# Building a state-space layer's Toeplitz matrices by a trip through DRAM, with the skip term folded into the lag matrix

## What is computed

```
def s5_mixer(h, w_in, ..., d_skip, w_glu):
    u = h @ w_in
    # per group of 16 channels, a complex state of 64:
    #   x[t] = a * x[t-1] + B @ u[t];   y[t] = Re(C @ x[t])
    y = y + d_skip * u
    g = gelu(y)
    val, gate = split(g @ w_glu, 2)
    return val * sigmoid(gate)
```

## Time and profile before

| | us |
|---|---|
| median of 3 runs | 2933.1 (2932.86 to 2935.42) |
| the profiled execution | 2935.41 |
| its span in the profile | 2933.6 |
| PE busy in the span | 2619.5 |
| DVE busy | 1939.3 |
| POOL busy | 1675.2 |
| ACT busy | 830.6 |

### The profile page before, as it was taken

One profiled execution on the slowest core, in us unless ns is written; L12 is line 12 of the kernel. 1 busy time (PEld: TensorE's weight loads), 2 busy tenths in 40 slices (PEclk: granted clock), 3 DMA queues, 4 the chain that ended last, 5 costly groups with the idle time before them and its releaser, 6 DMA issues.

```text
span 2933.6 us, 32517 instructions
## 1 busy us (share of the span) xinstructions
PE 2619.5 (89%) x9882; PEld 1218.3 (42%) x9882; DVE 1939.3 (66%) x3952; ACT 830.6 (28%) x1809; POOL 1675.2 (57%) x1024
## 2 busy tenths in 40 slices
PE   7989888888878888887778999999999988999999
PEld 3554333333333333332333684444444445444444
DVE  8847777777777777777877683666336596566523
ACT  3423222222222222222234461222112246222101
POOL 5544444444444444444535877777776651677776
PEclk9999999999999999999999979999999999999999
DMA  4259999999999999999972322233322320233332
GB/s 137 71 201 414 421 421 417 414 417 412 417 415 412 412 409 418 415 401 422 420 312 69 105 74 88 93 101 105 118 93 88 116 73 8 79 100 102 120 98 81
DMA packets 133244, 696.18 MB, mean 237 GB/s; under 512 B 30011, under 2 KB 31324, under 8 KB 67196
## 3 DMA queue, kind: packets, MB, share of 16 engines
q0 software_dynamic: 73728, 536.90, 44.5%
q1 hardware_dynamic: 59388, 157.74, 16.6%
HBM read 686.72 MB, written 7.86 MB: 237 GB/s over the span
## 4 chain that ended last, share of the span: by engine, by line
PE 34%; DMA 24%; POOLq 16%; DVE 12%; issue 7%; ACT 3%; DVEq 2%; POOL 1%; SPq 0%; ACTq 0%
DMA R<-expert_uv_dram,idx 24%; PE bank L586 20%; PE bank L814 9%; POOLq L2736 8%; POOLq L2734 7%; DVE R L2164 3%; POOL R L2761 1%; DVE Z L2186 1%; DVE xt L2449 1%; ACT Z L1437 1%; DVE R L1900 1%; PE bank L983 1%; PE bank L1170 1%; DVE R L2176 0%; DVE ci L2110 0%
## 5 line engine op out<-in xcount | busy, mean ns | idle before, releaser
L814 PE MATMUL bank<-R,Z 128*128 128x512 f32 x2048 | 971.4, 619 | 230.8 <-ACT Z L1437 225.3
L2761 POOL DMA_INDIRECT R<-expert_uv_dram,idx x512 | 596.5, 1165 | 723.7 <-PE bank L814 675.5
L586 PE MATMUL bank<-R 128*128 128x512 f16 (+1 forms) x3936 | 865.8, 381 | 6.6 <-DVE R L1882 2.6
L2164 DVE SCALAR_TENSOR_TENSOR R<-R 128x1024 f32<-128x1024 f32 x512 | 622.8, 1222 | 198.0 <-DMA R<-expert_uv_dram,idx 196.9
L814 PEld LDWEIGHTS bank<-R,Z 128*128 128x128 f32 x2048 | 381.6, 195 | 803.8 <-issue 420.5
L2733 POOL TENSOR_TENSOR R<-wring,beat 128x1024 f16<-128x1024 f32 (+2 forms) x219 | 447.2, 2042 | 394.7 <-PE bank L586 349.4
L586 PEld LDWEIGHTS bank<-R 128*128 128x128 f16 (+1 forms) x3936 | 383.7, 98 | 483.4 <-issue 25.3
L2735 POOL TENSOR_TENSOR R<-wring,R 128x1024 bf16<-128x1024 f32 (+2 forms) x219 | 510.2, 2330 | 31.8 <-issue 0.3
L1437 ACT ACTIVATE Z<-consts,R 128x128 f32<-128x128 f32 x512 | 177.7, 394 | 321.3 <-DVE R L2176 316.8
L586 PE MATMUL bank<-Z,R 128*128 128x512 f16 x1104 | 239.9, 379 | 1.5 <-POOLq L2736 1.5
L1430 ACT ACTIVATE R<-R 128x2 f32<-128x2 f32 x256 | 52.1, 204 | 608.3 <-DVEq L2166 607.9
(11 more groups left out here) (369 smaller groups left out, 2521.2 us busy)
## 6 DMA issues: line engine op xcount, KB each, us to landing
wring<-up_dram SPq DMA_DIRECT2D x88, 512.0 KB, 3.5
wring<-down_dram SPq DMA_DIRECT2D x32, 704.0 KB, 4.2
wring<-ple_dram SPq DMA_DIRECT2D x16, 640.0 KB, 3.9
wring<-w_in_dram SPq DMA_DIRECT2D x18, 512.0 KB, 3.5
R<-expert_uv_dram,idx POOLq DMA_INDIRECT x512
wring<-glu_dram SPq DMA_DIRECT2D x16, 512.0 KB, 4.2
Z<-w_q_dram SPq DMA_DIRECT2D x11, 512.0 KB, 8.0
wring<-ple_a_dram SPq DMA_DIRECT2D x8, 640.0 KB, 5.9
```

The costliest lines, as they stand in the source:

```text
L586: mm = pe.matmul(bank[:, :], low(w) if i else w, low(v) if j else v, start=(start and c == 0 and p == 0), stop=(stop and c == n - 1 and p ...
L814: mm = pe.matmul(banks[2 * par + c][:, :], diag[:, k % 4, :], pairs[:, slot, 1, c * SEQ:(c + 1) * SEQ], start=(k == 0), stop=(k == TOPK - 1))
L2164: dot = ve.scalar_tensor_tensor(pairs[:, slot, 0, :], pairs[:, slot, 0, :], 1.0, ntok[:, T, :], ALU.mult, ALU.mult, accum_out=act[:, par, ...
L2761: po.indirect_dma_start(pairs[:, slot, :, :].rearrange("p a b -> p (a b)"), None, A["expert_uv"], bass.IndirectOffsetOnAxis(idx[:, n % 2, ...
```

## The change

The shift products and their evictions are gone. The lag matrix goes from SBUF to DRAM (`lagD`) behind seven blocks of zeros, and one DMA with overlapping rows reads it back as Tg: row (j, c) starts j blocks further on. Powers 0 to 7 are now made in rising order, so that the u chunks are stored in reversed order, by eight DMAs per tile in place of one. The skip vector becomes a 16 x 128 matrix per tile, added to lag 0 by one product with 16 rows of the identity, ahead of the eight narrow products. `total` on DVE goes, and the gelu reads the landed y. The zeros are set in stage `final_a`, and two DMAs put them into DRAM. The copy that made the shift matrix is gone.

```diff
+        LAGS = (2 * CH - 1) * GC
+        lagD = nc.dram_tensor("lagD", [2, GC, GT, LAGS], F32, kind="Internal")
...
 SP, stage ssm_in
                     stream(name)
+                    for i, (at, n) in enumerate(((0, 2), (2, 2), (4, 4))):
+                        sp.dma_start(skips[i], A["ssm_skip"][:, at:at + n, :]).then_inc(d_loaded, 16)
+                    sp.wait_ge(ri_ready, NORM["ssm_in"] + 1)
+                    for slot in range(2):
+                        sp.dma_start(bass.AP(lagD, slot * P * LAGS, [[LAGS, P], [1, (CH - 1) * GC]]), pad)\
+                          .then_inc(d_loaded, 16)
...
-                        sp.dma_start(flat(uD, n).rearrange("(s p j) -> p s j", p=P, j=NCH),
-                                     uperm[:, n, :].rearrange("p (s j) -> p s j", j=NCH)).then_inc(u_stored[n % 2], 16)
+                        for i in range(CH):
+                            back = flat(uD, n)[(CH - 1 - i) * P * NCH:(CH - i) * P * NCH]
+                            sp.dma_start(back.rearrange("(p j) -> p j", j=NCH), uperm[:, n, i * NCH:(i + 1) * NCH])\
+                              .then_inc(u_stored[n % 2], 16)
...
 SP, stage ssm
                     stream("glu", ahead=True)
+                    def lags_out(n):
+                        sp.wait_ge(h_ev, n + 1)
+                        if n >= 2:
+                            sp.wait_ge(t_loaded, 16 * (n - 1))
+                        sp.dma_start(bass.AP(lagD, n % 2 * P * LAGS + (CH - 1) * GC,
+                                             [[GC, CH], [GT * LAGS, GC], [LAGS, GT], [1, GC]]),
+                                     hmat.rearrange("p (g m) -> p g m", m=GC)).then_inc(h_stored, 16)
+                    def lags_back(n):
+                        sp.wait_ge(h_stored, 16 * (n + 1))
+                        if n == 0:
+                            sp.wait_ge(d_loaded, 80)
+                        else:
+                            sp.wait_ge(t_loaded, 16 * n)
+                        if n >= 2:
+                            sp.wait_ge(y_mm, n - 1)
+                        sp.dma_start(Tg[:, n % 2, :, :],
+                                     bass.AP(lagD, n % 2 * P * LAGS, [[GC, CH], [GT * LAGS, GC], [LAGS, GT], [1, P]]))\
+                          .then_inc(t_loaded, 16)
+                    for n in range(2):
+                        lags_out(n)
+                        lags_back(n)
                     for n in range(KT):
+                        if n + 2 < KT:
+                            lags_out(n + 2)
+                            lags_back(n + 2)
                         sp.wait_ge(yo_ev, n + 1)
                         sp.dma_start(yD.ap()[n], ysb[:, n % 2, :]).then_inc(y_stored, 16)
...
 PE, stage ssm
                         if n:
-                            pe.wait_ge(te_ev, 2 * n - 1 + half)
+                            pe.wait_ge(bt_ev, 2 * n - 1 + half)
...
+                    pe.matmul(banks[2][:, 0:P], ident[0:GC, :], skip[n], start=True, stop=False)
                     for g in range(GT):
                         mm = pe.matmul(banks[2][:, g * GC:(g + 1) * GC], row(gmat[:, n % 2, g, :, :]),
-                                       Cm[:, n * GT + g, :], start=True, stop=True)
+                                       Cm[:, n * GT + g, :], start=False, stop=(g == GT - 1))
...
-                def output_matrices(n):
-                    pe.wait_ge(h_ev, n + 1)
-                    for half in range(2):
-                        pe.wait_ge(bt_ev, 2 * n + 1 + half)
-                        for j in range(4):
-                            at = (CH - 1 - half * 4 - j) * GC
-                            mm = pe.matmul(banks[half][:, j * P:(j + 1) * P], shifts[:, at:at + P], hmat,
-                                           start=True, stop=True)
-                        mm.then_inc(t_mm, 1)
...
                 def outputs(n):
-                    pe.wait_ge(te_ev, 2 * n + 2)
+                    pe.wait_ge(t_loaded, 16 * (n + 1))
...
 ACT, stage ssm
                     ac.wait_ge(h_mm, n + 1)
                     if n:
-                        ac.wait_ge(t_mm, 2 * n)
+                        ac.wait_ge(h_stored, 16 * n)
                     ac.activation(hmat, banks[2][:, 0:P], ACT.Copy).then_inc(h_ev, 1)
-                def output_matrices(n):
-                    if n >= 2:
-                        ac.wait_ge(y_mm, n - 1)
-                    for half in range(2):
-                        ac.wait_ge(t_mm, 2 * n + half + 1)
-                        ac.activation(Tg[:, n % 2, :, half * SEQ // 8:(half + 1) * SEQ // 8]
-                                      .rearrange("p g (t c) -> p t g c", c=GC),
-                                      banks[half][:, :].rearrange("p (t g c) -> p t g c", g=GT, c=GC),
-                                      ACT.Copy).then_inc(te_ev, 1)
...
 DVE
+                ve.memset(pad, 0.0)
...
-                ve.tensor_copy(shifts[:, 0:P], ident)
-                ve.memset(shifts[:, P:], 0.0)
...
-                def total(n):
-                    ve.wait_ge(tile_landed[n], 48)
-                    ve.scalar_tensor_tensor(uperm[:, n, :], uperm[:, n, :], col("ssm_d", n), uall[:, n, :],
-                                            ALU.mult, ALU.add).then_inc(y_total, 1)
...
 host
-    powers = np.concatenate([np.arange(CH - 1, -1, -1), np.arange(1, CH + 1)]).astype(f)
+    powers = np.concatenate([np.arange(CH), np.arange(1, CH + 1)]).astype(f)
+    lag0 = np.zeros((GC, KT, GT, GC), f)
+    for c in range(GC):
+        lag0[c, :, :, c] = g["ssm_d_2"][0].reshape(KT, GT, GC)[:, :, c]
+    out["ssm_skip"] = lag0.reshape(GC, KT, P)
```

More of the change, by code:

```diff
@@ L45 @@
                   ("conv_b_w", CONV_B * TB), ("ln_c_g", TC), ("ln_c_b", TC), ("b_s", HEADS_C), ("g_ffn", KT), ("g_ple", KT), ("g_final", KT), ("ssm_norm", KT),
-                  ("ssm_d", KT), ("kv_norm", KT), ("k_norm", 1), ("attn_norm", KT), ("q_norm", 1), ("subln", 1),
+                  ("kv_norm", KT), ("k_norm", 1), ("attn_norm", KT), ("q_norm", 1), ("subln", 1),
                   ("ffn_norm0", KT), ("ffn_norm1", KT), ("ffn_w0", 3 * 2 * FT), ("ffn_w1", 3 * 2 * FT),
@@ L299, in build @@
         gmat = view(R, 7168, 2, GT * CH * GC).rearrange("p b (g i c) -> p b g i c", i=CH, c=GC)
-        shifts = R[:, 10240:10240 + (2 * CH - 1) * GC]
+        skips = [R[0:GC, at:at + 2 * P].rearrange("c (b m) -> c b m", m=P) for at in (10240, 10688)] + \
+                [last_heads[0:GC, :].rearrange("c (b m) -> c b m", m=P)]
+        skip = [skips[0][:, 0, :], skips[0][:, 1, :], skips[1][:, 0, :], skips[1][:, 1, :]] + [skips[2][:, i, :] for i in range(4)]
+        pad = R[:, 14080:14080 + (CH - 1) * GC]
         hmat = R[:, 10496:10496 + P]
@@ L320, in build @@
             y_bank[:, i * GROUPS:(i + 1) * GROUPS] for i in range(7)]
-        [ssm_loaded, powers_ready, g_ready, e_ready, h_mm, h_ev, bt_mm, t_mm, bt_ev, te_ev, s_v_mm, vs_ready, decay_ready,
-         yv_ready, ys_ready, swap_used, x_ready, y_mm, yo_ev, y_stored, y_total, ph_ready, tab_ready, prep] = [
-            sem(n) for n in ("ssm_loaded", "powers_ready", "g_ready", "e_ready", "h_mm", "h_ev", "bt_mm", "t_mm", "bt_ev", "te_ev",
+        [ssm_loaded, powers_ready, g_ready, e_ready, h_mm, h_ev, bt_mm, h_stored, bt_ev, t_loaded, s_v_mm, vs_ready, decay_ready,
+         yv_ready, ys_ready, swap_used, x_ready, y_mm, yo_ev, y_stored, d_loaded, ph_ready, tab_ready, prep] = [
+            sem(n) for n in ("ssm_loaded", "powers_ready", "g_ready", "e_ready", "h_mm", "h_ev", "bt_mm", "h_stored", "bt_ev", "t_loaded",
                              "s_v_mm", "vs_ready", "decay_ready", "yv_ready", "ys_ready", "swap_used", "x_ready",
-                             "y_mm", "yo_ev", "y_stored", "y_total", "ph_ready", "tab_ready", "prep")]
+                             "y_mm", "yo_ev", "y_stored", "d_loaded", "ph_ready", "tab_ready", "prep")]
         u_stored = [sem(f"u_stored{i}") for i in range(2)]
@@ L507, in _ @@
                     stream(name)
+                    for i, (at, n) in enumerate(((0, 2), (2, 2), (4, 4))):
[4 more added lines that the diff above has]
+                          .then_inc(d_loaded, 16)
                     def chunks_back(n):
-                        sp.wait_ge(u_stored[n % 2], 16 * (n // 2 + 1))
+                        sp.wait_ge(u_stored[n % 2], 16 * CH * (n // 2 + 1))
                         sp.dma_start(uall[:, n, :], uD.ap()[n]).then_inc(tile_landed[n], 16)
@@ L970, in input_matrices @@
                         pe.wait_ge(h_ev, n)
+                    else:
+                        pe.wait_ge(d_loaded, 80)
+                    pe.matmul(banks[2][:, 0:P], ident[0:GC, :], skip[n], start=True, stop=False)
                     for g in range(GT):
                         mm = pe.matmul(banks[2][:, g * GC:(g + 1) * GC], row(gmat[:, n % 2, g, :, :]),
-                                       Cm[:, n * GT + g, :], start=True, stop=True)
```

(25 more changed lines are left out.)

## The result

The changed kernel takes 2965.4 us (2964.5 to 2966.6, five runs) against 2933.75 us: a ratio of 1.0108, 95% interval 1.0097 to 1.0119, so 31.7 us or 1.1% slower. I had forecast 2955 us and a range up to 2962. The direction and the mechanism held, the size was a third too small, and the range missed the result by 3.4 us.

The account below looks back on a forecast made before the run. PE was taken as the bound, at 1.2 GHz until the glu products: start at 1662.0 plus 108.4 us of input_matrices, outputs, chunk_inputs and tail puts glu 22 us later, so 2933.1 + 22 = 2955 us, range 2928 to 2962.

Parts of the forecast that it names:

- The clock: PE in stage ssm: low at 1.2 GHz from about 1648 us until the glu products; chance 0.72.
- The rivals with a returning clock: PE back at 2.4 GHz in the loop: throughout, 2923 us, chance 0.13; in some rounds, about 2938 us, chance 0.11.
- The start: Before the loop: input_matrices(2) begins 4.4 us earlier; outputs(0) waits zero to 1 us for the first Toeplitz matrix.
- The estimate for input_matrices(2): On PE, tile 2's input_matrices start at 1662.0 instead of 1666.36, once chunk_inputs(1) and gmat(2) are done.
- ACT may hold until about 1660: At the start, ACT's wait for the stored lag matrix ends about 1660, before chunk_inputs(1) ends.
- 3.2 us for seven more issues: SP's extra issue time behind the last tile; with 1.85 for the glu slabs, lags_out(0) comes near 1653.8.
- The price of a round: One tile's loop on PE at the low clock: 5.2 + 6.83 + 3.5 = 15.5 us.
- I take 0.2 us, since its weight load is hidden: The added skip product on PE, per tile: 0.2 us, bounds zero and 0.5 us.
- slow input_matrices: input_matrices on PE at the low clock: 5.0 us against 2.6 at the high one; bounds 2.6 and 5.6.
- The sum: Start of glu on PE: 1662.0 + 108.4 = 1770.4 against 1748.4 before, so +22.0 us.
- The transfer as a bound: Rival: the lag matrix's store takes over 11 us per round or Tg comes late; 12 us gives 2960 or more; chance 0.04.
- clock returns: Rival: PE at 2.4 GHz through the loop, POOL and DVE set an 11.6 us pace; 2923 us (2915 to 2926), chance 0.13.

Follow-up runs that it names:

- the filler: Changed kernel plus eight unread float32 products of ident by ident, 128 columns, per tile where the shift products stood; 2949.05 us, ratio 1.0054.
- the narrow experiment: Changed kernel plus eight unread products of ident by ident per tile where the shift products stood, 64 columns wide; 2987.97 us, ratio 1.0183.

## Why the prediction was right in its mechanism and short in its size

**The clock.** Right. The prediction read the earlier trace rows as "each recovery came with the very products that the change deletes"; the changed kernel stays at 0.50 from before 1651 us to the glu products, and two kernels with narrow products in that place do so too, while wide ones bring the clock back for a part of the stage. The rule of the Trainium skill that I had weighed against the rows ("TensorE: Matmul & The Clock Gate", section "Part 1: The HAM clock gate": sustained activity releases the throttle) did not decide here: 107 us without a pause at 1.2 GHz speak against it as I had read it. The rivals with a returning clock are out.

**The start.** The estimate for input_matrices(2), 1662.0, was met (1661.7), and by what it named: chunk_inputs(1) was done at 1661.1, and gmat, which POOL finished at 1661.6, released PE. What followed failed. PE waited 1.56 us for ACT's copy of the second lag matrix, which stood behind the first store, and 2.65 us for the first Toeplitz matrix: 4.2 us together, where the prediction had "zero to 1 us" for the second and nothing for the first ("ACT may hold until about 1660"; it held until 1664.9). Two terms of SP and its store were too small. "3.2 us for seven more issues" counted only the last tile. SP began its stores at 1619.3, when tiles 0 and 1 had long been copied out (it had been at the weight slabs before, as in the kernel before), paid 0.47 us for each of 64 issues, and never caught up: it reached the glu slabs at 1654.9, 6.2 us later than in the earlier trace rows, and the lag matrix at 1656.9 against my 1653.8. And the store took 7.9 us, not 5; the bound of 7.4 us was also too low.

**The price of a round.** 16.3 us instead of 15.5, and the step that failed is one term: "I take 0.2 us, since its weight load is hidden". The skip product costs 1.0 us, as its removal shows, twice even the upper bound of 0.5. Everything else in the round was priced right: slow input_matrices, 5.0 us, is 4.98 in the kernel without the product, outputs 6.86 against 6.83, chunk_inputs 3.4 against 3.5. Six times 0.8 us are 4.9 us.

**The sum.** The glu products began 31.1 us later, not 22. From 1661.7, 4.2 us of waits and 113.6 us of work give 1779.5; I had 1662.0 + 108.4. So 22.0 + 4.2 + 5.2 - 0.3 = 31.1: the waits at the start, and work that is nearly all skip product. The measured cost of that product lay outside its bounds, and so did the store; the range took only "a few us" for the start and left nothing for the product.

**The transfer as a bound.** Out for the loop: PE is busy for 106.28 of 107.10 us behind 1672.2, and none of its waits there is for a DMA. It counted once, at the start. But its price, 8.6 us per round and 11 at most, was too low. In the changed kernel SP's chain of store, load and y takes 14.2 us of a round (1705.25 to 1719.42), and in the run with wide products, where SP goes from one tile to the next without a wait, 11.8 us per tile (1689.49 to 1701.28 and to 1713.24). At 16.3 us a round that is hidden. With a clock at 2.4 GHz it would have been about as long as the 11.6 us that POOL and DVE need, which the rival "clock returns" did not reckon with.

**What was removed.** ACT and DVE lost their work as foreseen, and none of it reached the end: POOL alone waited 43.8 us for PE. At equal clock the change would be no loss on PE, SP's 11.8 us per tile left aside: at 2.4 GHz a round with the filler takes 10.4 us, of which the filler's block is 1.8, so 8.5 us are left, against a round of 9.8 us before (1682.3 to 1692.1 between two shift blocks of its timeline). That is worked out from two rows; no kernel ran the loop so at 2.4 GHz throughout.

## What to carry to other kernels

Before deleting matmuls from a stage of small products, cut the trace by granted clock and look at which instructions stand ahead of each recovery: here the deleted products, 1.8 us of a round, kept the other 8 us at double speed for much of the time. The kernel without them is 31 us slower, 22 us of it as the low clock was priced, and narrowing them alone cost 48 us. At the low clock price an added product as one that is not hidden until a row shows it: 16 rows by 128 columns cost 1.0 us. A DMA that replaces compute must be placed on its issuing queue from the first tile on, with the issue time of every new DMA before it (here 64 at 0.47 us) and what is already in flight. Padding with useless wide products is a way to test this, not a way to win.

## What the runs showed of the hardware that was not expected

TensorE stayed at 1.2 GHz for 107 us while its row in the profile was 99% busy, and for 153 us in the narrow experiment. Eight products per tile of equal count and place, 128 or 64 columns wide, decided between 2949 and 2988 us. One product with 16 rows added 1.0 us to a round at 1.2 GHz. With wide products added the clock could also alternate between its two levels with no idle time at all.

The changed kernel's DMA view (KB each, us to landing):

```profile
uD<-Z SPq DMA_DIRECT2D x64, 32.0 KB, 1.6
...
yD<-Z SPq DMA_DIRECT2D x8, 256.0 KB, 6.5
```

The store of y, 2.0 us in the earlier trace rows, took 6.5 when SP issued it right behind the load of a Toeplitz matrix (512 KB). The last two tiles have no such load ahead, and there it took 2.0 us in this kernel too (1771.53 to 1773.54 on SP). The store of a lag matrix, 64 KB in 64-byte runs, took 3.9 us with the slabs behind it, against 2.0 for the store of y, which is 256 KB in whole rows of 2 KB. The Trainium skill, "DMA: Bandwidth & Descriptors", section "Specifications", says that transfers below 512 bytes do not reach line rate; these numbers agree in direction.
